# One 512-column matmul for the high and low halves of x, the halves added on the way out of the bank

## What is computed

```
# layers a and b                              # layers sb and fox
z = rmsnorm(x) @ w_in                         z = rmsnorm(x) @ w_in
o = attention(z), memory_attention(z, mem)    o = attention(z)
x = x + o @ w_out                             x = x + rmsnorm(o @ w_out)
u = relu(rmsnorm(x) @ w_up)                   g, u = split(conv(rmsnorm(x) @ w_up))
x = x + (u * u) @ w_down                      x = x + rmsnorm((gelu(g) * u) @ w_down)
```

## Time and profile before

| what | value |
|---|---|
| three timed runs | 1382.49, 1388.46, 1389.96 us, median 1388.46 |
| span of the profiled execution, first to last instruction | 1383.6 us |
| median less span | 4.9 us |
| mean granted TensorE clock | 0.977 |
| busy: PE, weight loads, DVE, ACT, POOL | 96%, 89%, 68%, 53%, 34% |
| matmuls | 9952 |

### The profile page before, as it was taken

One profiled execution on the slowest core, in us unless ns is written; L12 is line 12 of the kernel. 1 busy time (PEld: TensorE's weight loads), 2 busy tenths in 40 slices (PEclk: granted clock), 3 DMA queues, 4 the chain that ended last, 5 costly groups with the idle time before them and its releaser, 6 DMA issues.

```text
span 1383.6 us, 29734 instructions
## 1 busy us (share of the span) xinstructions
PE 1329.8 (96%) x9952; PEld 1237.0 (89%) x9952; DVE 937.0 (68%) x1545; ACT 734.8 (53%) x1307; POOL 474.1 (34%) x465
## 2 busy tenths in 40 slices
PE   7998999999999999999999999999989999999996
PEld 7887899999986899999888689998979878999896
DVE  6587676655477666644678568997485555899844
ACT  6555554444454554444545556666464445666652
POOL 3122245300012245300202248886130003788811
PEclk9999899999999999999999799999999999999998
DMA  7543355555543255555543134555645314355462
GB/s 268 170 131 107 109 197 182 182 182 182 183 144 100 98 192 182 183 184 191 166 140 100 59 115 159 179 169 159 197 144 168 104 65 137 124 180 175 142 202 89
DMA packets 63286, 212.40 MB, mean 154 GB/s; under 512 B 7792, under 2 KB 8944, under 8 KB 62832
## 3 DMA queue, kind: packets, MB, share of 16 engines
q1 hardware_dynamic: 60912, 208.35, 46.3%
q10 hardware_dynamic: 2304, 3.15, 0.9%
HBM read 207.28 MB, written 1.05 MB: 151 GB/s over the span
## 4 chain that ended last, share of the span: by engine, by line
PE 40%; DVE 12%; POOL 7%; issue 4%; ACT 3%; DVEq 1%; POOLq 0%; ACTq 0%
PE bank L459 9%; PE bank L461 9%; PE bank L460 9%; POOL prod L1524 4%; DVE w_lo L1090 4%; DVE conv_buf L1194 3%; POOL conv_buf L1519 2%; PE bank L429 2%; PE bank L567 2%; PE bank L430 2%; PE bank L431 2%; PE bank L602 1%; DVE X L1226 1%; ACT a_hi L811 1%; DVE h_lo L1134 1%
## 5 line engine op out<-in xcount | busy, mean ns | idle before, releaser
L1090 DVE TENSOR_TENSOR w_lo<-raw,w_hi 128x1024 fp32r<-128x1024 f32 (+2 forms) x408 | 513.4, 1265 | 142.4 <-ACT w_hi L761 142.4
L761 ACT CAST w_hi<-raw 128x1024 fp32r<-128x1024 f32 (+2 forms) x408 | 407.4, 1003 | 287.3 <-PE bank L461 189.0
L459 PE MATMUL bank<-h_hi,w_hi 128*128 128x256 f32 x1168 | 335.0, 287 | 3.4 <-DVE w_lo L1090 3.3
L460 PE MATMUL bank<-h_lo,w_hi 128*128 128x256 f32 x1168 | 330.3, 283 | 0.0
L461 PE MATMUL bank<-h_hi,w_lo 128*128 128x256 f32 x1168 | 330.3, 283 | 0.0
L1455 POOL TENSOR_TENSOR sumsq<-sumsq,square 128x256 f32<-128x256 f32 x107 | 96.1, 898 | 491.3 <-ACT square L773 291.0
L459 PE MATMUL bank<-a_hi,w_hi 128*128 128x256 f32 x896 | 251.9, 281 | 10.4 <-DVE w_lo L1090 9.2
L460 PE MATMUL bank<-a_lo,w_hi 128*128 128x256 f32 x896 | 250.2, 279 | 0.0
L461 PE MATMUL bank<-a_hi,w_lo 128*128 128x256 f32 x896 | 250.1, 279 | 0.0
L459 PEld LDWEIGHTS bank<-h_hi,w_hi 128*128 128x128 f32 x1168 | 223.7, 192 | 10.3 <-issue 10.2
L460 PEld LDWEIGHTS bank<-h_lo,w_hi 128*128 128x128 f32 x1168 | 224.0, 192 | 0.1
(11 more groups left out here) (154 smaller groups left out, 2201.4 us busy)
## 6 DMA issues: line engine op xcount, KB each, us to landing
raw<-in_w_up_sb SPq DMA_DIRECT2D x44, 512.0 KB, 3.3
raw<-in_w_up_fox SPq DMA_DIRECT2D x44, 512.0 KB, 3.3
raw<-in_w_up_a SPq DMA_DIRECT2D x32, 512.0 KB, 3.3
raw<-in_w_down_a SPq DMA_DIRECT2D x32, 512.0 KB, 4.5
raw<-in_w_up_b SPq DMA_DIRECT2D x32, 512.0 KB, 3.3
raw<-in_w_down_b SPq DMA_DIRECT2D x32, 512.0 KB, 4.3
raw<-in_w_in_sb SPq DMA_DIRECT2D x24, 512.0 KB, 3.4
raw<-in_w_in_fox SPq DMA_DIRECT2D x24, 512.0 KB, 4.4
```

The lines of the kernel that those rows point to most:

```text
L459: nc.tensor.matmul(dst, w_hi[:, slot, w], src_hi[:, at + k, :], start=begin, stop=False)
L460: nc.tensor.matmul(dst, w_hi[:, slot, w], src_lo[:, at + k, :], start=False, stop=False)
L761: nc.scalar.copy(w_hi[:, slot, 0:k * P], raw[:, slot, 0:k * P]).then_inc(hi_ready, 1)
L1090: nc.vector.tensor_tensor(w_lo[:, slot, 0:k * P], raw[:, slot, 0:k * P], w_hi[:, slot, 0:k * P].bitcast(f32), ALU.subtract).then_inc(lo_re ...
```

## The change

The high and low halves of each activation lie in one tensor (`h1[:, 0]` and `h1[:, 1]`, likewise `h2`, `a_both`, `o_both`). `product` issues one matmul of w_hi with 512 moving columns, x_hi and x_lo side by side, into a whole bank, and one of w_lo with x_hi into its first 256 columns. The two halves of the bank are added as the tile is taken out: ACT copies the second half to SBUF and DVE adds the first (`copy_low`, `join`), or DVE adds both in turn (`residual`). up_sb and up_fox (`TOGETHER`), the values and the forget gate's logits keep three matmuls.

First PE's part, then ACT's, then DVE's:

```diff
+            def product(both, slot, k, at, src, first, last):
+                w = slice(k * P, (k + 1) * P)
+                def wide():
+                    return nc.tensor.matmul(both, w_hi[:, slot, w], src[:, :, at, :], start=first, stop=last)
+                def narrow():
+                    return nc.tensor.matmul(both[:, 0:TOK], w_lo[:, slot, w], src[:, 0, at, :], start=False,
+                                            stop=False)
+                if first:
+                    wide()
+                    return narrow()
+                narrow()
+                return wide()
...
-                    nc.tensor.matmul(dst, w_hi[:, slot, w], src_hi[:, k, :], start=k == 0, stop=False)
-                    nc.tensor.matmul(dst, w_hi[:, slot, w], src_lo[:, k, :], start=False, stop=False)
-                    last = nc.tensor.matmul(dst, w_lo[:, slot, w], src_hi[:, k, :], start=False, stop=k == KT - 1)
+                    last = product(bank[s % 2][:], unit % RING, k, k, src, k == 0, k == KT - 1)
```

```diff
+            def copy_low(dst, both):
+                nc.scalar.copy(dst, both[:, TOK:2 * TOK]).then_inc(low_copied, 1)
+            def take_low(name, dst):
+                per = plan[name]["body"]
+                def tile(i, done, b, first):
+                    act.wait_ge(units_done, done)
+                    if name in DOWN_OF.values():
+                        act.wait_ge(a_ready, i * 4 + (PRODUCTS[name] + b + 1))
+                    if name == "mem_a":
+                        act.wait_ge(h_lo, operand_count("mem_b", 0, 0, KT - 1))
+                    at = b if dst is u_buf else i * per + b
+                    copy_low(dst[:, at, :], bank[b])
+                return tile
             def output_tile(name, norm, g):
                 per = plan[name]["body"]
                 def tile(i, done, b, first):
-                    act.wait_ge(units_done, done)
-                    squared(norm, bank[b][:, 0:TOK], i, per, b)
-                    nc.scalar.activation(H[:, i * per + b, :], bank[b][:, 0:TOK], ACT.Identity,
-                                         scale=gain(g, i * per + b)).then_inc(tile_out, 1)
+                    act.wait_ge(tile_out, i * per + (plan[name]["tile"] + b + 1))
+                    at = i * (per * TOK) + b * TOK
+                    y = H[:].rearrange("p k t -> p (k t)")[:, bass.ds(at, TOK)]
+                    squared(norm, y, i, per, b)
+                    nc.scalar.activation(y, y, ACT.Identity,
+                                         scale=gain(g, i * per + b))
...
             def query_key_tile(name, s):
                 g = plan[name]
-                split(0, RING, g["unit"] + g["values"] + s + RING, KT)
+                unit, memory = g["unit"] + g["values"] + s, s - (g["tiles"] - g["values"])
+                act.wait_ge(units_done, unit + 1)
+                copy_low(Z[:, s, :] if memory < 0 else ZM[:, 4 + memory, :], bank[s % 2])
+                split(0, RING, unit + RING, KT)
...
-            project("up_a", after=relu("up_a"), middle=norm_scale)
+            project("up_a", before=take_low("up_a", u_buf), after=relu("up_a"), middle=norm_scale)
-            project("out_sb", before=output_tile("out_sb", "post_sb", "sb_post_g_2"))
+            project("out_sb", before=take_low("out_sb", H),
+                    after=output_tile("out_sb", "post_sb", "sb_post_g_2"))
```

```diff
+            def join(dst, both, name, at):
+                dve.wait_ge(low_copied, at + (COPIED[name] + 1))
+                nc.vector.tensor_tensor(dst, both[:, 0:TOK], dst, ALU.add).then_inc(halves_joined, 1)
+                dve.wait_ge(halves_joined, at + (JOINED[name] + 1))
             def query_key_tile(name, s):
...
-                nc.vector.tensor_tensor(dst, bank[s % 2][:, 0:TOK], scale[:], ALU.mult).then_inc(tile_out, 1)
+                join(dst, bank[s % 2], name, s)
+                nc.vector.tensor_tensor(dst, dst, scale[:], ALU.mult).then_inc(tile_out, 1)
                 split(0, RING, unit + RING - 1, KT)
...
             def residual(name, operands):
-                    nc.vector.tensor_tensor(x, bank[b][:, 0:TOK], x, ALU.add).then_inc(tile_out, 1)
+                    nc.vector.tensor_tensor(x, bank[b][:, 0:TOK], x, ALU.add).then_inc(half_added, 1)
+                    dve.wait_ge(half_added, i * per + (ADDED[name] + b + 1))
+                    nc.vector.tensor_tensor(x, bank[b][:, TOK:2 * TOK], x, ALU.add).then_inc(tile_out, 1)
...
             def relu(name):
-                    nc.vector.scalar_tensor_tensor(u_buf[:, b, :], bank[b][:, 0:TOK], 0.0, rstd[:], ALU.max,
+                    join(u_buf[:, b, :], bank[b], name, i * 4 + b)
+                    nc.vector.scalar_tensor_tensor(u_buf[:, b, :], u_buf[:, b, :], 0.0, rstd[:], ALU.max,
                                                    ALU.mult).then_inc(tile_out, 1)
...
+            def output_tile(name):
+                    dve.wait_ge(units_done, done)
+                    dve.wait_ge(low_copied, i * per + (COPIED[name] + b + 1))
+                    y = H[:, i * per + b, :]
+                    nc.vector.tensor_tensor(y, bank[b][:, 0:TOK], y, ALU.add).then_inc(tile_out, 1)
```

More of the change, by code:

```diff
@@ L292, in build_program, with tiles_before @@
         TOGETHER = ("up_sb", "up_fox")
+        def tiles_before(names):
+            before, count = {}, 0
+            for name in names:
+                before[name] = count
+                count += plan[name]["tiles"] - plan[name]["values"]
+            return before
+        COPIED = tiles_before(["mem_a", "in_a", "mem_b", "up_a", "in_b", "up_b", "in_sb", "out_sb", "down_sb", "in_fox",
+                               "out_fox", "down_fox"])
+        JOINED = tiles_before(["mem_a", "in_a", "mem_b", "up_a", "in_b", "up_b", "in_sb", "in_fox"])
+        ADDED = tiles_before(["out_a", "down_a", "out_b", "down_b"])
         DIRECT = ("final", "post_sb", "post_ffn_sb", "post_fox", "post_ffn_fox")
@@ L458, in trip @@
                                 pe.wait_ge(h_lo, operand_count(name, 0, 0, k))
[L459 to L462, removed]
+                            if name in TOGETHER:
+                                w, dst = slice(k * P, (k + 1) * P), bank[b][:, 0:TOK]
+                                nc.tensor.matmul(dst, w_hi[:, slot, w], src[:, 0, k, :], start=begin, stop=False)
+                                nc.tensor.matmul(dst, w_hi[:, slot, w], src[:, 1, k, :], start=False, stop=False)
+                                last = nc.tensor.matmul(dst, w_lo[:, slot, w], src[:, 0, k, :], start=False,
+                                                        stop=end)
+                            else:
+                                last = product(bank[b][:], slot, k, at + k, src, begin, end)
                         last.then_inc(units_done, 1)
@@ L639, in _ @@
             keep_warm(log_ms, 20)
-            gemm("mem_a", a_hi, a_lo)
+            gemm("mem_a", a_both)
             pe.wait_ge(consts_in, 16 * len(CONSTS))
@@ L643, in _ @@
             transpose_values(ZM, 2, 2)
[L645 to L649, removed]
+            fused("in_a", lambda s: query_key_tile("in_a", s, h1 if s < 2 + 2 * ROPE_PAIRS else h2), attention("in_a"), 4)
+            gemm("out_a", o_both, attended("in_a"))
+            gemm("up_a", h2)
+            gemm("down_a", a_both)
             values("in_b")
@@ L652, in _ @@
             pe.wait_ge(h_lo, operand_count("q_b", 0, 0, KT - 1))
-            fused("in_b", lambda s: query_key_tile("in_b", s, *((h1_hi, h1_lo) if s > 2 and s % 2
-                                                                else (h2_hi, h2_lo))), attention("in_b"), 3)
-            gemm("out_b", o_hi, o_lo, attended("in_b"))
-            gemm("up_b", h2_hi, h2_lo)
-            gemm("down_b", a_hi, a_lo)
+            fused("in_b", lambda s: query_key_tile("in_b", s, h1 if s > 2 and s % 2 else h2), attention("in_b"), 3)
+            gemm("out_b", o_both, attended("in_b"))
+            gemm("up_b", h2)
+            gemm("down_b", a_both)
             mean_square()
@@ L661, in _ @@
             values("in_sb")
-            fused("in_sb", lambda s: query_key_tile("in_sb", s, h1_hi, h1_lo), attention("in_sb"), 4)
-            gemm("out_sb", o_hi, o_lo, attended("in_sb"))
+            fused("in_sb", lambda s: query_key_tile("in_sb", s, h1), attention("in_sb"), 4)
+            gemm("out_sb", o_both, attended("in_sb"))
             mean_square()
             keep_warm(ones, 7)
-            gemm("up_sb", h2_hi, h2_lo)
-            gemm("down_sb", a_hi, a_lo)
+            gemm("up_sb", h2)
+            gemm("down_sb", a_both)
             mean_square()
@@ L1022, in _ @@
             act.wait_ge(a_ready, RING)
-            project("mem_a", middle=norm_scale)
+            project("mem_a", before=take_low("mem_a", ZM), middle=norm_scale)
             for k in range(KT):
@@ L1051, in _ @@
             nc.scalar.preload_act_table_set("natural_log_exp_and_others")
[L1052 removed]
```

(2 more changed lines are left out.)

66 lines of the change are left out of this document (35 added, 31 removed).

## The result

Slower: 1453.28 us (median of 5 runs, 1446.73 to 1454.41) against 1389.96 for before on the same chip, a ratio of 1.0475, 95% interval 1.0454 to 1.0496. The direction was forecast, the size was not: 1417 was the number and 1440 the end of the range. The profiled execution has a span of 1444.9 us, 61.3 more than before, where the sum had 28.9; it took 1446.73, the least of its five runs, so the median stands 8.4 above the span, not 4.9. The miss of 36 is 32.4 of span and 3.5 of this.

What follows compares the result with a forecast made beforehand. It took PE, 96% busy, as paced by columns plus 0.009 to 0.013 per matmul, with DVE bounding out_a. Terms sum to +28.9 on a span of 1383.6, 1412.5; with 4.9 for the median, 1417, range 1392 to 1440.

Steps and rivals of the forecast that it cites:

- the sum: Whole kernel: all stage terms added make +28.9 us on a span of 1383.6.
- What PE gains: PE, 2176 products: two matmuls for three, each gaining 0.0088 with a and o operands or 0.0132 with h.
- the first rival: Attention loops: DVE's waits cover the join, so PE's gain wins, -18 us, 1370; chance 0.08.
- in_a, in_b, in_sb, in_fox: Fused attention stages: copy and join lengthen the ACT-DVE loops, +9.9, +5.6, +6.4; in_fox's cover holds, -0.8.
- The multiplications beside POOL: 12 rotating pairs: multiplications reading SBUF can be held up by POOL, up to 1 us each, +12, 1429.
- the third rival: Worse than the sum: POOL holds up the multiplications and PE's gaps lower its clock, 1430 to 1445; chance 0.12.
- out_a and up_a (and _b): Second add in out, then DVE's loop through POOL with the join, 2.99 per tile: +5.4 for each layer.
- The +3.1: Turn from out_a: the second add on eight tiles, less waits, makes up_a start 3.1 late.
- The w_lo lead: End of up_a and up_b: w_lo's lead of three units hides 3.5 of the lateness.
- up_sb and up_fox at nothing: up_sb and up_fox: they don't change in form, so no cost was forecast.
- The rest: mem_a's last tile +0.9; out and down of sb and fox -4.2, their tails +3.9; together +0.6.
- cancelling: Attention stages keep PE's pace (-7) and the up stages pay: 1388 to 1392; chance 0.07.

Runs made afterwards that it cites:

- experiment 1: Kernel before with the change's wide matmuls and joint tensors but the old take-out, so w_hi x_lo is never read: 1385.81 us, 1.0008 of before.
- experiment 2: Changed kernel with its whole take-out but three narrow matmuls, only each tile's first product wide: 1456.25 us, 1.0521 of before.
- experiment 5: Kernel before with only the change's joint tensors, narrow matmuls and old take-out everywhere: 1395.72 us, 1.0063 of before.
- Experiment 4: Changed kernel with mem_a and the four fused attention stages as before in everything: 1419.99 us, 1.0257 of before.
- experiment 7: Changed kernel with the low half in the four fused attention stages copied by DVE instead of ACT: 1430.03 us, 1.031 of before.
- experiment 12: Kernel before with wide matmuls and the new take-out in up_a and up_b alone, a_hi and a_lo apart, no moved a_lo: 1398.09 us, 1.0087 of before.
- experiment 8: Kernel before with wide matmuls in up_a and up_b alone, a_lo moved behind the next join, a_hi and a_lo apart: 1381.97 us, 0.9954 of before.
- experiment 9: Kernel before, three narrow matmuls, with only a_lo in up_a and up_b moved behind the next tile's take-out: 1387.48 us, 1.0002 of before.
- experiment 6: Changed kernel with a_lo in up_a and up_b moved between the next tile's join and its multiplication: 1427.92 us, 1.0306 of before.

## Why the prediction was right and wrong, step by step

**What PE gains** was mis-sized. The step took 0.2268 for a wide matmul from the values stage, where wide follows wide. Between narrow ones it takes 0.230 to 0.235, and more than 0.23 is what the prediction itself named as a sign of its being wrong. A product gains 0.011 with h operands in the up stages (forecast 0.0132), but 0.003 with a operands (forecast 0.0088). All of it is worth 6 to 8 us (experiments 1, 2 and 5), not the 24 that 2176 x 0.011 makes in the first rival. down_a and down_b gave back 0.5 each over seven of their eight tiles; the sum had 3.6 for the two stages, so 2.6 of the miss is here.

**in_a, in_b, in_sb, in_fox** were right in mechanism, and by the landmarks nearly in size. The stages up to out_a are 13.1 late (forecast 9.9 + 0.9), in_b adds 7.0 from down_a's last residual to out_b's first (5.6), in_sb 5.3 between its tiles (6.4), and in_fox is 0.2 shorter between its first and last tile. Experiment 4 puts them all, with mem_a, at 30 by the ratios, 29 by the span, against 22 in the sum, so they are under-priced by up to 8; experiment 7 shows that the place in ACT's queue is the larger part.

**The multiplications beside POOL** were a part of the third rival: up to 1 us on each of 12 pairs. The multiplication that the row above shows took 1.01 instead of 0.42, and three others in in_a 1.29 to 1.34; over all 64 the mean is 0.49 against 0.42. But the w_lo splits, 1.30 to 2.26 in six of the steps of in_a before, are all 1.22 or less after (the row is before's):

```profile
115.07 2.26 DVE L1090 TENSOR_TENSOR w_lo<-raw,w_hi 128x1024 fp32r<-128x1024 f32 x1
```

The hold moved from one DVE instruction to another: over in_a it draws the splits out by 4.2 before and the multiplications by 3.3 after. The Trainium skill (SBUF — State Buffer, "SBUF: two separate sides") says that of a DVE instruction with two SBUF inputs and a GpSimd one that reads SBUF the one that starts first holds the port for the whole instruction and the other waits. The trace agrees: in up_sb the one that starts 0.04 later is the one that takes 0.45 or 0.25 longer.

**out_a and up_a (and _b)** is the step that failed most, by 12.9 of the 32.4. It had the loop right (2.99, measured 3.03) and four sizes wrong.

- The turn: the second add costs 2.8 in out_a, near the forecast, but the step went from there straight to PE's start. The +3.1 has PE's stand in it (2.69), but the lowered clock behind the stand was in no term. From the last h2_lo to the first take-out it takes 196.64 - 188.78 = 7.86, against 178.64 - 172.38 = 6.26 before; of these 1.6 some 0.4 are ACT's copy of the tile.
- The trip's end, 0.3 on every fourth tile, had been hidden behind PE before (every tile 2.88). There DVE's recorded instructions have the loop's counter and its branch between `a_lo` and the next join. It stays in experiment 12 (3.28 for 2.99), with a_hi and a_lo apart, so it isn't the layout's. Between first and last tile up_a lost 7.7 for the forecast 5.8.
- up_b lost 9.7 there. These 2.0 more go with the joining of a_hi and a_lo too: in up_b, and not in up_a, a register instruction stands ahead of three `a_lo` in four, and the tiles take 3.10 and the trip's end 3.53, for 3.03 and 3.31. In experiment 12, with a_hi and a_lo apart and without these instructions, the two stages are alike (91.5 and 91.8).
- The w_lo lead gave back 1.7 at the stage's end (26.2 less the join's own 0.46, against 24.0), not 3.5.

**up_sb and up_fox at nothing** was wrong by 8.1, and shown to be the layout (experiment 5), and of it the joining of a_hi and a_lo: experiments 8, 9 and 12 keep the other joint tensors and have 126.1 to 126.3. The prediction read the change's new tensors as a matter of names, and asked no view what slack these stages had; there DVE is the bound at 91%.

**The rest:** from up_sb's last tile to in_fox's first it takes 3.8 more than before, for a forecast near 0. Of this 2.1 belongs to the profiled execution of before: in it 3 matmuls of down_sb took 0.340, while experiments 5, 8 and 9, whose down_sb is as before, need 102.1 for this stretch against 100.1 there. Most of the rest is the clock, an estimate: in after its mean is 0.92 over the first 21 us of the stretch, where these three have 1.00, and 0.08 of 21 is 1.7. Experiment 12, also with down_sb as before, has the same 0.92 and needs 103.4, so it isn't the edit of down_sb that brings it.

**The rivals.** That PE's gain wins was ruled out, as was cancelling. The third rival, worse than the sum, had 0.12 and was what happened, but not for its reasons: one of the two (the clock) is a small part, the other (POOL beside the multiplications) none, and its 1445 was still short. The Trainium skill's rule on weight loads (Perfetto Trace Analysis, "Identifying the Most-Contended Engine", which takes their busy share and the share of peak FLOPs as TensorE's measures of headroom) did not help: with PE's part alone their busy share fell from 89% to 81%, and the time changed by half a per cent (experiments 1 and 5).

## What to carry to other kernels

Price an added instruction by the loop that it joins: an engine's idle time in a loop is cover only if the new instruction may run in it, and then reordering is worth more than the instruction costs (experiments 6, 8 and 12). Follow every lateness on to the next engine that has to wait for it, and look at what its clock does after the wait. When tensors are merged, count the register instructions of the engines that address them in loops where such an engine is the bound, even in stages that the change leaves alone.

## What the runs showed of the hardware that was not expected

Joining two tensors (experiment 5) cost 0.6% of the whole time with the same computation. By the trace a single register instruction on DVE, 0.08 us (the idle time ahead of `a_lo` is 0.59 against 0.51), settled once in a trip of 12 us whether POOL is held (0.88 for 0.63) or DVE (0.88 for 0.43). A matmul of 512 columns between two of 256 takes 0.230 to 0.235 from start to start, against 0.227 among its like. Matmuls of the same form took 0.113 each in down_sb and 0.118 in its twin down_fox, in one execution of before; no run explains it.
